# First norm of a decoder layer in two halves of 264 tokens: input loads, clears and first products in another order

## The reference, cut to what matters

```python
h = jnp.concatenate([meta, x], axis=1)              # 528 x 1024
h = h + 0.5 * swiglu(rmsnorm(h, ffn1_norm), w_gate, w_up, w_down)   # D_FF = 2816
h = h + token_mixing(rmsnorm(h, mix_norm), w_in, ..., w_out, ...)
h = h + 0.5 * swiglu(rmsnorm(h, ffn2_norm), ...)
out = rmsnorm(h, final_norm)[:, 16:]

def rmsnorm(x, g): return x * lax.rsqrt(jnp.mean(x * x, -1) + EPS) * g
def swiglu(h, g, u, d): return (jax.nn.silu(h @ g) * (h @ u)) @ d
```

## Time and profile before

| what | us |
|---|---|
| median of 3 runs (1035.13 to 1035.25) | 1035.2 |
| the profiled execution's own time | 1035.24 |
| its span in the profile | 1033.5 |
| PE busy | 1025.8 (99%) |
| DVE busy | 739.6 (72%) |
| ACT busy | 541.0 (52%) |
| POOL busy | 463.6 (45%) |

### The profile page before, as it was taken

One profiled execution on the slowest core, in us unless ns is written; L12 is line 12 of the kernel. 1 busy time (PEld: TensorE's weight loads), 2 busy tenths in 40 slices (PEclk: granted clock), 3 DMA queues, 4 the chain that ended last, 5 costly groups with the idle time before them and its releaser, 6 DMA issues.

```text
span 1033.5 us, 20282 instructions
## 1 busy us (share of the span) xinstructions
PE 1025.8 (99%) x7693; PEld 951.3 (92%) x7693; DVE 739.6 (72%) x1292; ACT 541.0 (52%) x891; POOL 463.6 (45%) x571
## 2 busy tenths in 40 slices
PE   9999999999999999999999999999999999999997
PEld 9999999999999999889878788878899999999997
DVE  7877667787665588599975585578877766666735
ACT  7665545445454354562556526544555554554536
POOL 5344335344343367259931304455444433433440
PEclk9999999999999999999999999999999999999999
DMA  8788777777876444335320102222767887777732
GB/s 225 141 185 187 165 174 153 167 163 159 187 147 148 135 114 117 90 93 143 94 81 24 52 12 82 66 76 84 174 142 167 182 179 178 164 168 179 154 91 82
DMA packets 195108, 137.54 MB, mean 133 GB/s; under 512 B 8643, under 2 KB 179702, under 8 KB 195014
## 3 DMA queue, kind: packets, MB, share of 16 engines
q1 hardware_dynamic: 178208, 97.38, 33.7%
q0 software_dynamic: 16704, 38.80, 22.4%
q10 hardware_dynamic: 102, 0.08, 0.0%
HBM read 91.18 MB, written 2.10 MB: 90 GB/s over the span
## 4 chain that ended last, share of the span: by engine, by line
PE 89%; issue 5%; DVE 4%; ACT 1%; DVEq 0%; POOL 0%; ACTq 0%; POOLq 0%
PE ps L2667 38%; PE ps L2902 37%; PE ps L633 4%; PE ps L2709 2%; PE ps L780 1%; PE ps L810 1%; PE ps L831 1%; DVE mask L1490 1%; DVE small L1486 1%; PE ps L951 1%; PE ps L715 1%; PE ps L2956 0%; PE ps L2932 0%; PE ps L843 0%; DVE mask L1459 0%
## 5 line engine op out<-in xcount | busy, mean ns | idle before, releaser
L1912 POOL TENSOR_TENSOR wl<-raw,wh 128x256 fp32r<-128x256 f32 x196 | 154.2, 836 | 187.5 <-ACT wh L2069 133.0
L1940 POOL DMA_DIRECT2D wxl<-raw x78 | 66.7, 856 | 248.0 <-ACT wxl L2074 246.9
L2667 PE MATMUL ps<-ah,wxh 128*128 128x264 f32 (+2 forms) x464 | 123.3, 319 | 0.1
L2667 PE MATMUL ps<-ah,wxl 128*128 128x264 f32 (+2 forms) x464 | 123.0, 318 | 0.0
L2667 PE MATMUL ps<-al,wxh 128*128 128x264 f32 (+2 forms) x464 | 122.9, 318 | 0.0
L2667 PE MATMUL ps<-xh,wh 128*128 128x264 f32 (+3 forms) x400 | 114.0, 334 | 0.0
L2667 PE MATMUL ps<-xl,wh 128*128 128x264 f32 (+3 forms) x400 | 110.5, 325 | 0.0
L2667 PE MATMUL ps<-xh,wl 128*128 128x264 f32 (+3 forms) x400 | 110.2, 324 | 0.0
L2902 PE MATMUL ps<-xh,wh 128*128 128x264 f32 (+1 forms) x380 | 107.5, 283 | 0.0
L2902 PE MATMUL ps<-xl,wh 128*128 128x264 f32 (+1 forms) x380 | 107.5, 283 | 0.0
L2902 PE MATMUL ps<-xh,wl 128*128 128x264 f32 (+1 forms) x380 | 107.2, 282 | 0.0
(11 more groups left out here) (334 smaller groups left out, 3058.8 us busy)
## 6 DMA issues: line engine op xcount, KB each, us to landing
raw<-in_ffn_w_gate SPq DMA_DIRECT2D x44, 512.0 KB, 5.1
raw<-in_ffn_w_up SPq DMA_DIRECT2D x44, 512.0 KB, 5.5
raw<-in_ffn_w_down SPq DMA_DIRECT2D x80, 256.0 KB, 4.0
wxl<-raw POOLq DMA_DIRECT2D x60, 256.0 KB, 3.9
raw<-in_w_in SPq DMA_DIRECT2D x28, 512.0 KB, 4.2
wxl<-raw POOLq DMA_DIRECT2D x21, 512.0 KB, 5.2
wl<-raw POOLq DMA_DIRECT2D x19, 512.0 KB, 5.2
raw<-in_w_out SPq DMA_DIRECT2D x8, 512.0 KB, 3.4
```

The source lines that it names most:

```text
L1912: op = pool.tensor_tensor(dst[:, part], src[:, part], high[:, part].bitcast(F32), ALU.subtract)
L1940: pool.dma_start(places(1, PLACE[u], c)[:, 0:n], raw[:, u % RING, 0:n], accum_op=ALU.add).then_inc(low_added[e], 16)
L2667: mm = pe.matmul(ps[0:m, bank + a, 0:width], places(lo, PLACE[u], -(-WIDTH[u] // HALF_UNIT))[:, k * P:k * P + m], r[:, tile, t:t + width], ...
```

## The change

The norm of the input is done in two halves of 264 tokens. Each half has its own root, its own spread, and its own `xn`, `xh` and `xl` instructions (8 tiles x 264 columns instead of 8 x 528), and the first products are ordered by token half. With it go these edits:

- SP loads the first gate unit after two tiles of x instead of four.
- PE runs 8 matmuls on ones at the start instead of 10, and none behind the spread. Turns 6 and 7 stand behind the first spread, turns 8 and 9 inside the products. Turns 8 and 9 are both copied by ACT. The second half's diagonals are made by DVE, those of tiles 1 and 2 by ACT, that of tile 0 by POOL.
- POOL rounds both first units (ACT rounded the second), and makes the low part of each right behind.
- DVE's order is `xn` of half 0, two copies, the second root, two diagonals, `xl` of half 0, `xn` of half 1, `xl` of half 1. PE starts half 1 when `h_done` is set, behind `xn` of half 1.
- DVE forms the low part of "t3" between the first plain product and its low part; ACT loads the table of silu before it waits for the sums of x.
- In the attention loop one filling step stands ahead of `turn_probs` for the four pairs with a spread; the tails stand one filling step earlier. In the linear attention's output ACT's root takes the scale and EPS, and DVE inverts behind it, so one DVE instruction a window is gone.

The diff, cut to its core (lines taken out that the code above shows are left out where they are many):

```diff
-        X_BANKS, VEC_BANK = 6, 4
-        X_BY_ACT = 8
+        X_BANK, VEC_BANK = [0, 1, 2, 3, 4, 5, 4, 5, 1, 3], 7
...
+                if p > 1:
+                    values(p - 1)
+                fill_first = p == 1 or p > 4 and p % 4 == 2
+                if fill_first:
+                    fill_step(KT + 2 * p)
                 if p == 1:
-                    fill_step(KT + 2 * p)
-                if p:
                     values(p - 1)
                 for n in (2 * p, 2 * p + 1):
                     turn_probs(n, TURNS.index((True, n)))
-                if p != 1:
+                if not fill_first:
...
             def root_o(w):
-                act.wait_ge(o_inv, 2 * (w + 1))
-                act.activation(o_r[:, w, :], o_r[:, w, :], ACT.Sqrt).then_inc(o_rstd, 1)
+                act.wait_ge(o_sum, w + 1)
+                act.activation(o_r[:, w, :], o_ssq[:, w, :], ACT.Sqrt, bias=eps, scale=1.0 / DV).then_inc(o_rstd, 1)
...
-                dve.wait_ge(o_sum, w + 1)
-                dve.tensor_scalar(o_r[:, w, :], o_ssq[:, w, :], 1.0 / DV, EPS, ALU.mult, ALU.add).then_inc(o_inv, 1)
-                dve.wait_ge(o_inv, 2 * w + 1)
+                dve.wait_ge(o_rstd, w + 1)
                 dve.reciprocal(o_r[:, w, :], o_r[:, w, :]).then_inc(o_inv, 1)
             def gate_out(w):
-                dve.wait_ge(o_rstd, w + 1)
+                dve.wait_ge(o_inv, w + 1)
                 for hd in range(GLA_HEADS):
...
+                            load_x(2)
+                            load_x(3)
...
-            pool.wait_ge(w_in_slot[0], 16)
-            for c in range(0, UNIT, SHORT):
-                op = pool.tensor_copy(places(0, PLACE[0], 2)[:, c:c + SHORT], raw[:, 0, c:c + SHORT])
-            op.then_inc(w_hi, 2)
+            pool.tensor_tensor(diag[:, 0, :], ident[:, :], xvar[:, 0:1].broadcast_to([P, P]), ALU.mult).then_inc(x_diag_pool, 1)
+            def half_of(u, c):
+                return slice(c * HALF_UNIT, (c + 1) * HALF_UNIT), places(0, PLACE[u], 2)
+            def hi_half(u, c):
+                part, high = half_of(u, c)
+                for a in range(part.start, part.stop, SHORT):
+                    op = pool.tensor_copy(high[:, a:a + SHORT], raw[:, u, a:a + SHORT])
+                op.then_inc(w_hi, 1)
             def lo_half(u, c):
-                part = slice(c * HALF_UNIT, (c + 1) * HALF_UNIT)
+                part, high = half_of(u, c)
                 pool.wait_ge(w_hi, Q_HI[u] - 1 + c)
...
+                low(places(1, PLACE[u], 2)[:, part], raw[:, u, part], high[:, part], 1)
+            for u in range(2):
+                pool.wait_ge(w_in_slot[u], 16)
+                for c in range(2):
+                    hi_half(u, c)
+                for c in range(2):
+                    lo_half(u, c)
             pool.wait_ge(c_zero, 2)
             pool.affine_select(out=tri[:, :], in_=tri[:, :], compare_op=ALU.is_ge, fill=NEG, base=0,
...
+            def high_x(half, d):
+                part = slice(half * HALF, (half + 1) * HALF)
+                act.wait_ge(xn_done, KT * half + d + 1)
+                act.activation(xh[:, d, part], xn[:, d // 4, 4 + d % 4, part], ACT.Copy).then_inc(x_hi, 1)
+            x_square(1)
+            x_square(2)
+            x_roots(0)
+            act.wait_ge(x_inv, 2)
+            act.wait_ge(x_turned, 6)
+            for t in range(1, 3):
+                act.activation(diag[:, t, :], ident[:, :], ACT.Copy, scale=xvar[:, t:t + 1]).then_inc(x_diag, 1)
+            x_square(3)
+            for d in range(4):
+                high_x(0, d)
+            x_square(4)
             x_roots(1)
...
+            for d in range(4, KT):
+                high_x(0, d)
+            for n in X_BY_ACT:
+                keep_x(act, n)
+            act.wait_ge(w_hi, Q_HI[1])
+            hi(2)
             for d in range(KT):
...
+                high_x(1, d)
+            negative(2)
             hi(3)
-            negative(2)
             negative(3)
             ffn(U_FFN1, 0, 0)
...
                         dve.tensor_tensor(as_parts(t1[:, tk], norm), as_parts(t0[:, tk], norm), psum_parts(4 * (j % 2) + 2, norm),
                                           ALU.mult).then_inc(a_prod, 1)
                         dve.wait_ge(a_prod, j + 1)
+                        if between:
+                            x_low(between)
                         low(t1[:, tk], j, ft + j + 1)
-                    dve.wait_ge(x_lo, KT)
-                    dve.wait_ge(xn_done, KT)
+                    dve.wait_ge(x_lo, 2 * KT)
+                    dve.wait_ge(xn_done, 2 * KT)
                     x_sums(True)
                     x_sums(False)
                     sums(U_PAIR[number, 1, 0])
                     x_low("t2")
-                    plain_product(0)
+                    plain_product(0, "t3")
                     low_pair(U_PAIR[number, 1, 0])
-                    x_low("t3")
                     x_low("t1")
...
-                if n == 3:
-                    invert_x(0)
-                if n == 6:
-                    invert_x(1)
+            for n in range(3):
+                keep_x(dve, n)
+            invert_x(0)
+            for n in range(3, 6):
+                keep_x(dve, n)
             dve.wait_ge(vecs_turned, 1)
             dve.tensor_copy(vecs[:, :], ps[:, VEC_BANK, 0:4 * KT + 3]).then_inc(vecs_kept, 1)
-            dve.wait_ge(x_kept, 9)
-            dve.wait_ge(x_kept_act, 1)
+            dve.wait_ge(vecs_kept, 1)
+            def norm_x(half):
+                part = slice(half * HALF, (half + 1) * HALF)
+                dve.wait_ge(x_kept, 6 + 2 * half)
+                if half:
+                    dve.wait_ge(x_kept_act, 2)
+                dve.wait_ge(x_spread, half + 1)
+                for d in range(KT):
+                    dve.scalar_tensor_tensor(out=xn[:, d // 4, 4 + d % 4, part], in0=h[:, d, part],
+                                             scalar=gains[:, 0, d:d + 1], in1=ps[:, 6 + half, 0:HALF], op0=ALU.mult,
+                                             op1=ALU.mult).then_inc(xn_done, 1)
+            def low_x(half):
+                part = slice(half * HALF, (half + 1) * HALF)
+                for d in range(KT):
+                    dve.wait_ge(x_hi, KT * half + d + 1)
+                    dve.tensor_tensor(xl[:, d, part], xn[:, d // 4, 4 + d % 4, part], xh[:, d, part].bitcast(F32),
+                                      ALU.subtract).then_inc(x_lo, 1)
+            norm_x(0)
+            keep_x(dve, 6)
+            keep_x(dve, 7)
+            invert_x(1)
+            dve.wait_ge(x_inv, 3)
+            for t in range(3, 5):
+                dve.tensor_scalar(diag[:, t, :], ident[:, :], xvar[:, t:t + 1], None, ALU.mult).then_inc(x_diag, 1)
+            low_x(0)
+            norm_x(1)
+            dve.wait_ge(x_kept, 8)
+            dve.wait_ge(x_kept_act, 2)
             dve.sem_inc(h_done, KT)
...
+            low_x(1)
             ffn(U_FFN1, 0, 0)
             invert(1)
...
+                def parts(v, lo, low_x, half):
+                    for k in range(KT):
+                        mm = part(v, k, lo, low_x, half)
                     return mm
-                def low_inputs(v):
-                    for k in range(KT):
-                        mm = part(v, k, 0, True)
+                pe.wait_ge(x_kept, 3)
+                for k in range(4):
+                    part(0, k, 0, False, 0)
+                for k in range(2):
+                    part(0, k, 1, False, 0)
+                turn_x(8)
+                turn_x(9)
+                for k in range(2, 4):
+                    part(0, k, 1, False, 0)
+                for k in range(4, KT):
+                    part(0, k, 0, False, 0)
+                    part(0, k, 1, False, 0)
+                parts(1, 0, False, 0)
+                spread(1)
+                parts(0, 0, True, 0)
+                parts(1, 1, False, 0)
+                parts(1, 0, True, 0)
+                pe.wait_ge(x_kept, 7)
+                parts(2, 0, False, 0)
+                pe.wait_ge(h_done, KT)
+                for k in range(KT):
+                    for v in range(2):
+                        for lo in range(2):
+                            part(v, k, lo, False, 1)
+                parts(2, 0, False, 1)
+                parts(0, 0, True, 1).then_inc(w_used, 2)
+                parts(1, 0, True, 1).then_inc(w_used, 2)
+                pe.wait_ge(xn_done, 2 * KT)
+                parts(3, 0, False, 0)
+                parts(3, 0, False, 1)
+                for v in (2, 3):
+                    for half in range(2):
+                        parts(v, 1, False, half)
+                    for half in range(2):
+                        mm = parts(v, 0, True, half)
                     mm.then_inc(w_used, 2)
...
+            def turn_x(n):
                 t, half = X_TURNS[n // 2], n % 2
                 w = x_cols(n)[1]
                 pe.wait_ge(x_loaded[t], 16)
-                if n >= X_BANKS:
```

(27 more changed lines are left out.)

132 lines of the change are left out of this document (26 added, 106 removed).

## The result

| | median us | runs | profiled execution, span |
|---|---|---|---|
| before | 1035.31 | 14, 1035.13 to 1035.63 | 1035.24, 1033.5 |
| changed | 1037.71 | 14, 1037.17 to 1038.99 | 1037.84, 1036.0 |

A forecast was written before the change was run, and what follows sets the result against it. The prediction took PE as the bound (89% of the span ends on it). Its terms, 2.0 - 0.23 - 0.27 + 0.1 = +1.6 us, took the profiled 1035.24 to 1036.8, with a range from 1033.9 to 1038.0.

The forecast's parts named there:

- term 1: At the start, up to the paired products: DVE's and POOL's order makes PE finish the first products 2.0 us later.
- 25 us: At the start: the forecast is wrong if half 1 starts before 22 us or after 25.
- `xn` of half 0 at 10.1: At the start, on DVE: `xn` of half 0 starts at 10.1 us instead of 12.49, 2.4 us gained.
- DVE and POOL take turns, `xl` ends at 20.2: At the start: `xl` of half 0 alternates with POOL's low parts, each costing DVE some 0.6 us, ending near 20.2.
- PE ready at 23.2, half 1 at 23.3: At the start: PE finishes its earlier matmuls at 23.2 us, as `h_done` is set at 23.3, then 136 matmuls follow.
- slow clock: Rival, 13%: PE falls to the slow clock, the first 3 us behind `h_done` at half speed, 1.5 us more, 1038.3.
- Term 2: Behind the first products: PE's wait for DVE's `al` at 43.13 us goes away, -0.23 us.
- the DMA additions land before they are wanted: Behind the first products: additions of units 2 and 3 wanted behind 31 us; first pair's lands near 35, wanted at 39.8.
- Term 3: In the mixer's output, first window: PE's wait for DVE near 637 us goes away, -0.27 us.
- Term 4: In the attention loop: waits for ACT's copy covered, -0.7, but splitting filling steps costs 0.8, so +0.1 us.
- The slow clock at the start: PE's turns before the change: passes start 7 to the us at 5 us, read as 1.2 GHz, against 11 at 9.
- no-lock rival: Rival, 27%: POOL's low parts do not hold up DVE, `xl` of half 0 ends below 18.3 us, 1034.3.

## Why the prediction was right, and where its numbers were not

The side was right, and so was the mechanism of term 1: the head start is lost because half 1's `xn` stands behind half 0's `xl` and POOL's low parts. The experiments show that mechanism: with the block out of DVE's way the first diagonal, or whatever stands first, no longer waits, and half 1's `xn` starts at 18.1 to 18.2 instead of 20.40. The time lies inside the range, 0.9 us above the forecast, and with 0.22% just past the bound of 0.2%, for which the prediction gave 25%. Terms 1, 3 and 4 were off in size, and half 1's start at 24.85 is just short of the 25 us that the prediction named as a sign against itself.

- *`xn` of half 0 at 10.1*: 10.39. *Half 1's `xn` behind half 0's `xl`*: yes, from 20.40.
- *DVE and POOL take turns, `xl` ends at 20.2*: the turns were wrong, the end was nearly right (20.4). DVE stood through three more of POOL's instructions, then ran alone. The sum of the work is the same in either order, so the joint end moved little, as the prediction said. The Trainium skill (page SBUF — State Buffer, section "SBUF: two separate sides") has a lock per instruction, and whoever comes second is blocked; the traces agree with blocking (2.55 and 2.87 us where 0.28 and 0.42 is usual). That one instruction can be passed over by three of the other's is what the runs add. `xn` again ran beside POOL's low parts at full pace: 3.29 us from 10.39 beside them, 3.28 from 20.40 with POOL idle.
- *PE ready at 23.2, half 1 at 23.3*: PE came at 24.85, while `h_done` was there at 23.65. This is the mis-sized term. The last `xl` product started at some 20.8 instead of 20.3, and the 24 matmuls behind it took 3.9 us instead of 2.9, at half clock. So in the traced execution the 13% rival "slow clock" happened on top of the forecast, ahead of `h_done` and not behind it; in most executions there was no such fall. That the median moves so little with it fits the table above: the addition lands at 45.7 in any case, and PE reaches that place at 45.82 even with the fall. The prediction had looked at the additions of units 2 and 3 and at the first pair's, but not at this next one, issued at 36.90 before and at 39.81 now. Term 1 was 2.0 and measured 3.67, 1.55 of the rest in this step, the other 0.1 in the 136 matmuls (16.61 against 16.5).
- *Term 2, -0.23*: in the changed kernel the lag falls by 0.31 there, so its number held, by luck: it did so because PE was late enough to hide the addition. Alone the edits cost 0.57. The step that failed is that the DMA additions land before they are wanted: it counted when they are issued, not what is issued in front of them.
- *Term 3, -0.27*: 0.26 at the first window and 0.04 behind it in the kernel with this edit alone; 0.45 in the changed one, where the attention's edits are in too. Right for its place.
- *Term 4, +0.1*: 0.36 were gained. The waits it named are gone; a split of the filling steps costs some 0.04 us at the two that show it alone, not 0.2. The tails one step earlier were put at nothing; the medians of the two kernels differ by 0.3, but their traces show no cost behind that edit, so the 0.3 is open.
- *The slow clock at the start*: the prediction read a slow clock at 5 us from the pace of the passes (7 to the us against 11). The column of the granted clock shows 1.00 in both stretches, as it said, so no row here shows the lower level there.
- *Sum*: 3.67 - 0.31 - 0.36 - 0.45 = 2.5 in the spans, 2.4 in the medians, against 1.6. The near agreement of the total owes something to luck: term 1 was 1.7 too small, and terms 3 and 4 gave 0.6 more than forecast.

The no-lock rival named 18.3 us as its limit; `xl` ended at 18.2 only once POOL's block was moved, and then the pairs were at 38.45, not 37.3: half 1 starts at 21.81, not 20.8, since PE's products up to 15 us wait for ACT's `xh`, and behind them 0.38 for the low weights. So a start in halves, in the orders tried, is no gain in this kernel even then (pairs at 38.45 against 37.79). The version to keep is the old start with the new attention order and root, 1034.05.

## What to carry to other kernels

Before splitting a stage in halves, follow the second half's first instruction: here it stood behind the first half's last, and the head start was void. Where one step frees a buffer earlier, look at which DMA is issued by it and what it now overtakes; 1 MB of loads in front of a small transfer that is waited for cost more here than the stall that the step took away (0.57 us more in all, for a stall of 0.28). A trace is one execution; where a cause such as the clock can come and go, the list of all executions says how much of the median it can carry. And where several bounds lie within a microsecond, an early gain has to be followed to the next wait before it is booked.

## What the runs showed of the hardware

- An instruction of DVE that starts under a row of POOL's low parts waited for the whole row of three more (2.55, 2.57 and 2.87 us, three kernels), whatever its form; in the row at 35 us before it waited for one. A cast between the low parts let it in. What decides between waiting for one and waiting for three isn't settled.
- The granted clock fell to 1.2 GHz where PE had waited and was then fed one matmul per 0.34 us; it fell as well with a wait of 0.43 us in place of 1.09, and did not fall in the kernel in which PE stood for 1.11 and 0.63 us, nor in the one with casts and low parts in turn, where six `xl` products came every 0.35 us behind a wait of 0.38, nor with matmuls of ones between. Each of these is one traced execution, and executions of the changed kernel differ in it (0.997 to 1.0 as the mean granted clock). What decides isn't settled. The Trainium skill (page TensorE: Matmul & The Clock Gate, section "What's actually happening") has activity release the throttle; the runs agree in that the matmuls of ones kept the granted clock at 1.00.
- An addition by DMA of 128 KB lands 3.3 us after its issue with 1 MB of loads issued 0.7 us behind it, and 5.9 us with the same loads issued 0.5 us ahead; over the trace of the kernel before, 4.5 to 8.0 us with two loads issued up to 0.9 us ahead (nineteen additions) and 2.7 to 4.9 us with them 0.7 to 1.7 us behind (ten).
